# A two-block transformer kernel: the loaded tiles stand 520 bytes apart in place of 512

## What is computed

```python
def swiglu(h, w13, w2):
    gate, up = jnp.split(h @ w13, 2, axis=-1)
    return (jax.nn.silu(gate) * up) @ w2
...
    def expert_block(args):
        tok_b, e_b = args
        xb = x2[tok_b]
        return swiglu_2(xb, w1[e_b], w3[e_b], w2[e_b])
...
    y_blk = lax.map(expert_block, (buf_tok.reshape(NB, MOE_BLOCK), blk_e))
    y = y_blk.reshape(P, D) * buf_g[:, None]
    return jnp.zeros((T, D), x2.dtype).at[buf_tok].add(y)
```

## Time and profile before

| | |
|---|---|
| median of 3 runs | 3226.8 us |
| lowest, highest | 3224.2, 3227.34 us |
| the profiled execution | 3226.32 us |
| its span in the trace | 3224.4 us |
| granted TensorE clock, mean | 0.994 of full |
| PE busy | 3141.2 us, 97% of the span |
| PEld, DVE, ACT, POOL busy | 90%, 64%, 53%, 45% |

### The profile page before, as it was taken

How to read it: one execution, slowest core, us unless ns; L and a number is a source line. 1 busy time by engine, 2 the same in 40 slices (tenths; PEclk the granted TensorE clock), 3 DMA queues, 4 the chain that set the end, 5 groups by cost and what they waited for, 6 DMA issues and landing times.

```text
span 3224.4 us, 53354 instructions
## 1 busy us (share of the span) xinstructions
PE 3141.2 (97%) x20750; PEld 2887.8 (90%) x20750; DVE 2069.5 (64%) x2086; ACT 1722.8 (53%) x2031; POOL 1463.3 (45%) x587
## 2 busy tenths in 40 slices
PE   8999999999999999999999999999999999999998
PEld 8998999998789989899999998898888888888887
DVE  6644654734534376273644572657999999998997
ACT  5343444443234344644433555546777777777775
POOL 7864687882048755488888764691000000000000
PEclk9999999999999999999999999999999999999999
DMA  6443554553245443345455443356998989988985
GB/s 239 177 155 122 182 182 157 183 182 144 92 140 183 167 149 128 134 151 189 170 182 183 164 150 144 118 188 242 379 347 339 381 345 344 378 339 344 384 341 219
DMA packets 97230, 704.30 MB, mean 218 GB/s; under 512 B 10928, under 2 KB 10928, under 8 KB 11600
## 3 DMA queue, kind: packets, MB, share of 16 engines
q1 hardware_dynamic: 96768, 700.26, 58.4%
q10 hardware_dynamic: 288, 2.10, 0.2%
q0 software_dynamic: 48, 0.13, 0.0%
HBM read 701.40 MB, written 1.05 MB: 218 GB/s over the span
## 4 chain that ended last, share of the span: by engine, by line
PE 84%; DVE 7%; POOL 4%; issue 3%; ACT 2%; DVEq 0%; DMA 0%; POOLq 0%; ACTq 0%
PE bank L646 23%; PE bank L648 23%; PE bank L647 23%; POOL half_lo L608 4%; PE bank L771 3%; DVE kept L2423 2%; PE bank L1119 2%; PE bank L768 1%; PE bank L736 1%; PE bank L1261 1%; DVE expert_parts L2597 1%; PE bank L1307 1%; PE bank L889 1%; PE bank L923 1%; PE bank L785 1%
## 5 line engine op out<-in xcount | busy, mean ns | idle before, releaser
L608 POOL TENSOR_TENSOR half_lo<-ring,half_hi 128x1024 fp32r<-128x1024 f32 x582 | 1462.4, 2520 | 725.7 <-ACT half_hi L1393 721.5
L1393 ACT ACTIVATE half_hi<-ring 128x1024 fp32r<-128x1024 f32 x582 | 612.7, 1057 | 815.1 <-PE bank L648 752.1
L646 PE MATMUL bank<-h_hi,half_hi 128*128 128x256 f32 x2928 | 838.5, 286 | 10.4 <-POOL half_lo L608 10.4
L647 PE MATMUL bank<-h_lo,half_hi 128*128 128x256 f32 x2928 | 829.8, 283 | 0.0
L648 PE MATMUL bank<-h_hi,half_lo 128*128 128x256 f32 x2928 | 829.8, 283 | 0.0
L646 PEld LDWEIGHTS bank<-h_hi,half_hi 128*128 128x128 f32 x2928 | 563.3, 192 | 16.6 <-issue 8.0
L647 PEld LDWEIGHTS bank<-h_lo,half_hi 128*128 128x128 f32 x2928 | 563.3, 192 | 0.7
L648 PEld LDWEIGHTS bank<-h_hi,half_lo 128*128 128x128 f32 x2928 | 563.1, 192 | 0.0
L1846 ACT ACTIVATE expert_parts<-ring 128x1024 fp32r<-128x1024 f32 x336 | 337.3, 1055 | 109.6 <-PE bank L648 109.6
L646 PE MATMUL bank<-expert_parts,h_hi 128*128 128x512 f32 x896 | 355.1, 396 | 6.7 <-DVE expert_parts L2597 5.3
L648 PE MATMUL bank<-expert_parts,h_hi 128*128 128x512 f32 x896 | 349.9, 391 | 0.0
(11 more groups left out here) (400 smaller groups left out, 5536.7 us busy)
## 6 DMA issues: line engine op xcount, KB each, us to landing
ring<-stream SPq DMA_DIRECT2D x327, 1024.0 KB, 4.8
ring<-experts SPq DMA_DIRECT2D x168, 1024.0 KB, 6.6
kept<-experts SPq DMA_DIRECT2D x112, 1024.0 KB, 7.0
lent<-experts SPq DMA_DIRECT2D x56, 1024.0 KB, 6.8
lent<-mem ACTq DMA_DIRECT2D x2, 1024.0 KB, 6.9
con<-consts SPq DMA_DIRECT2D x1, 1505.0 KB, 12.0
kept<-x_in SPq DMA_DIRECT2D x1, 1024.0 KB, 5.0
kept<-mem SPq DMA_DIRECT2D x1, 1024.0 KB, 16.1
```

The costliest lines, as they stand in the source:

```text
L608: nc.gpsimd.tensor_tensor(half_lo[:, h % HALVES, :], ring[:, u % RING, s * HALF:(s + 1) * HALF], half_hi[:, h % HALVES, :].bitcast(F32), A ...
L646: mm(dst, w_hi, x_hi, start=start, stop=False, skip_group_check=shared)
L647: mm(dst, w_hi, x_lo, start=False, stop=False, skip_group_check=shared)
L1393: nc.scalar.activation(half_hi[:, h % HALVES, :], ring[:, u % RING, s * HALF:(s + 1) * HALF], ACT.Copy).then_inc(hi_ready, 1)
```

## The change

Three row lengths are new: `WROW` is 130 floats, `SROW` 130, and `XROW` 256, which leaves it as it was. The tiles in `half_hi` and `half_lo` stand 130 floats (520 bytes) apart in place of 128, and so do the experts' stationary tiles in `h_hi` and `h_lo`. Two floats after each tile are not used. The number of instructions, their order on each engine, their waits and their element counts stay the same. What is written to these tiles (L1393, L608, `turned`) is written in eight or four rows of 128 in place of one row of 1024 or 512; where a half moves, it moves as two rows of 128.

The tiles' starts are now spread over the multiples of 8 bytes: tile k starts 8k bytes further than before, counted from the first tile of its tensor. The tensors grow by 192 bytes each (`half_hi`, `half_lo`) and 128 bytes each (`h_hi`, `h_lo`), so what stands behind them moves too: seen modulo 512 bytes, `half_lo` starts at 192, `h_hi` at 384, `h_lo` at 0, `hid_hi`, `hid_lo`, `lent` and `expert_parts` at 128.

```diff
+WROW, XROW, SROW = PARTS + 2, TOK + 0, SLOTS + 2
...
-        half_hi = sb("half_hi", [PARTS, HALVES, HALF], F32R)
-        half_lo = sb("half_lo", [PARTS, HALVES, HALF], F32R)
-        h_hi = sb("h_hi", [PARTS, KT, TOK], F32R)
-        h_lo = sb("h_lo", [PARTS, KT, TOK], F32R)
+        half_rows = [sb(name, [PARTS, HALVES * 8 * WROW], F32R) for name in ("half_hi", "half_lo")]
+        half_hi, half_lo = (a[:, :].rearrange("p (h k c) -> p h k c", h=HALVES, k=8)[:, :, :, 0:PARTS] for a in half_rows)
+        h_rows = [sb(name, [PARTS, max(KT * XROW, 16 * SROW)], F32R) for name in ("h_hi", "h_lo")]
+        h_hi, h_lo = (a[:, 0:KT * XROW].rearrange("p (k t) -> p k t", k=KT)[:, :, 0:TOK] for a in h_rows)
...
+        slot_rows = [a[:, 0:16 * SROW].rearrange("p (k s) -> p k s", k=16)[:, :, 0:SLOTS] for a in h_rows]
+        xs_hi, xs_lo = (slot_rows[0][:, KT * i:KT * (i + 1), :] for i in range(2))
+        hT_hi, hT_lo = ([slot_rows[1][:, KT * i + 4 * j:KT * i + 4 * (j + 1), :] for j in range(2)] for i in range(2))
...
+        def by_tile(a):
+
+            return a.rearrange("p (k c) -> p k c", c=PARTS)
...
-                    nc.gpsimd.tensor_tensor(half_lo[:, h % HALVES, :], ring[:, u % RING, s * HALF:(s + 1) * HALF],
-                                            half_hi[:, h % HALVES, :].bitcast(F32), ALU.subtract).then_inc(lo_ready, 1)
+                    nc.gpsimd.tensor_tensor(half_lo[:, h % HALVES, :, :], by_tile(ring[:, u % RING, s * HALF:(s + 1) * HALF]),
+                                            half_hi[:, h % HALVES, :, :].bitcast(F32), ALU.subtract).then_inc(lo_ready, 1)
...
-                        cols = slice(k * PARTS, (k + 1) * PARTS)
-                        last = products(b[:, m * 256:m * 256 + 256], w_hi[:, cols], w_lo[:, cols], h_hi[:, k, :],
+                        last = products(b[:, m * 256:m * 256 + 256], w_hi[:, k, :], w_lo[:, k, :], h_hi[:, k, :],
                                         h_lo[:, k, :], k == 0, k == KT - 1)
...
-                            last = products(bank[5 + s][:, :], hT_hi[:, i % 2, rows_k], hT_lo[:, i % 2, rows_k],
+                            last = products(bank[5 + s][:, :], hT_hi[i % 2][:, k, :], hT_lo[i % 2][:, k, :],
                                             hi[:, cols], lo[:, cols], i == 0 and k == 0, i == NCHUNK - 1 and k == 3)
...
-                nc.scalar.activation(half_hi[:, h % HALVES, :], ring[:, u % RING, s * HALF:(s + 1) * HALF],
+                nc.scalar.activation(half_hi[:, h % HALVES, :, :], by_tile(ring[:, u % RING, s * HALF:(s + 1) * HALF]),
                                      ACT.Copy).then_inc(hi_ready, 1)
```

More of the change, by code:

```diff
@@ L515, in two_blocks @@
         onehot = page(7, 4, SLOTS)
-        scat, gate_slot = half_hi[:, 0, 0:TOK], small[:, 0:1]
+        scat, gate_slot = half_rows[0][:, 0:TOK], small[:, 0:1]
         ye_hi, ye_lo = (a[:, :, :].rearrange("p a b -> p (a b)") for a in (hid_hi, hid_lo))
         scat_bank = (2, 4, 5, 6)
[L520 to L523, removed]
+        slot_rows = [a[:, 0:16 * SROW].rearrange("p (k s) -> p k s", k=16)[:, :, 0:SLOTS] for a in h_rows]
+        xs_hi, xs_lo = (slot_rows[0][:, KT * i:KT * (i + 1), :] for i in range(2))
+        hT_hi, hT_lo = ([slot_rows[1][:, KT * i + 4 * j:KT * i + 4 * (j + 1), :] for j in range(2)] for i in range(2))
         expert_ring = [ring[:, i, :] for i in range(RING)] + [page_of[i][:, 0:UNIT] for i in (6, 9, 2)]
@@ L527, in two_blocks @@
         w_lo = [expert_parts[:, RING * UNIT:(RING + 1) * UNIT], expert_parts[:, (RING + 1) * UNIT:(RING + 2) * UNIT],
-                half_lo[:, 0:2, :].rearrange("p h c -> p (h c)")]
+                half_rows[1][:, 0:2 * HALF]]
+        def by_tile(a):
+            return a.rearrange("p (k c) -> p k c", c=PARTS)
         @block.sync
@@ L641, in half @@
                 pe.wait_ge(lo_ready, 2 * BODY * r + (h + 1))
-                return half_hi[:, h % HALVES, :], half_lo[:, h % HALVES, :]
+                return half_hi[:, h % HALVES, :, :], half_lo[:, h % HALVES, :, :]
             def products(dst, w_hi, w_lo, x_hi, x_lo, start, stop, shared=False):
@@ L674, in parted @@
                             if token_major:
-                                toks, cols = slice(m * PARTS, (m + 1) * PARTS), slice(i * 256, (i + 1) * 256)
-                                last = products(dst, x_hi[k][:, toks], x_lo[k][:, toks], w_hi[:, cols], w_lo[:, cols],
+                                toks, cols = slice(m * PARTS, (m + 1) * PARTS), slice(2 * i, 2 * i + 2)
+                                last = products(by_tile(dst), x_hi[k][:, toks], x_lo[k][:, toks], w_hi[:, cols, :], w_lo[:, cols, :],
                                                 start, stop, True)
                             else:
-                                cols = slice(i * 256 + m * PARTS, i * 256 + (m + 1) * PARTS)
-                                last = products(dst, w_hi[:, cols], w_lo[:, cols], x_hi[k], x_lo[k],
+                                last = products(dst, w_hi[:, 2 * i + m, :], w_lo[:, 2 * i + m, :], x_hi[k], x_lo[k],
                                                 start, stop, True)
@@ L703, in opening @@
                                 pe.wait_ge(xg_hi, k // 2 + 1)
-                            mm(b[:, m * 256:m * 256 + 256], half_hi[:, h % HALVES, k * PARTS:(k + 1) * PARTS], h_hi[:, k, :],
+                            mm(b[:, m * 256:m * 256 + 256], half_hi[:, h % HALVES, k, :], h_hi[:, k, :],
                                start=k == 0 and m == 0, stop=False, skip_group_check=True)
@@ L710, in opening @@
                             pe.wait_ge(xg_hi, 4 * n - 4 + k // 2 + 1)
-                        cols = slice(k * PARTS, (k + 1) * PARTS)
                         dst = b[:, m * 256:m * 256 + 256]
                         if n > 1:
-                            mm(dst, w_hi[:, cols], h_hi[:, k, :], start=k == 0 and m == 0, stop=False, skip_group_check=True)
-                        mm(dst, w_lo[:, cols], h_hi[:, k, :], start=False, stop=False, skip_group_check=True)
+                            mm(dst, w_hi[:, k, :], h_hi[:, k, :], start=k == 0 and m == 0, stop=False, skip_group_check=True)
+                        mm(dst, w_lo[:, k, :], h_hi[:, k, :], start=False, stop=False, skip_group_check=True)
                 for i, (b, u, m) in enumerate(parts):
@@ L720, in opening @@
                             pe.wait_ge(xg_lo, 4 * n - 4 + k // 2 + 1)
-                        last = mm(b[:, m * 256:m * 256 + 256], w_hi[:, k * PARTS:(k + 1) * PARTS], h_lo[:, k, :],
+                        last = mm(b[:, m * 256:m * 256 + 256], w_hi[:, k, :], h_lo[:, k, :],
                                   start=False, stop=k == KT - 1, skip_group_check=True)
@@ L823, in down @@
                         for m in range(KT):
-                            cols = slice(m * PARTS, (m + 1) * PARTS)
-                            last = products(bank[4 + m // 2][:, (m % 2) * 256:(m % 2) * 256 + 256], w_hi[:, cols], w_lo[:, cols],
+                            last = products(bank[4 + m // 2][:, (m % 2) * 256:(m % 2) * 256 + 256], w_hi[:, m, :], w_lo[:, m, :],
                                             hid_hi[:, i % 2, k * 256:(k + 1) * 256], hid_lo[:, i % 2, k * 256:(k + 1) * 256],
@@ L1889, in turned @@
                     act.wait_ge(ht_done, NCHUNK * n + 2 * c + (i + 1))
-                    nc.scalar.activation(hT_hi[:, i % 2, :], bank[4][:, :], ACT.Copy).then_inc(ht_hi_ready, 1)
+                    nc.scalar.activation(hT_hi[i % 2], by_tile(bank[4][:, :]), ACT.Copy).then_inc(ht_hi_ready, 1)
                 def chunk(i, c=0):
```

3 lines of the change are left out of this document (1 added, 2 removed).

## The result

| | before | after |
|---|---|---|
| median of 3 runs | 3226.8 us | 3203.81 us |
| lowest, highest | 3224.2, 3227.34 us | 3203.32, 3204.37 us |
| span of the profiled execution | 3224.4 us | 3201.5 us |

The ratio is 0.9931, with a 95% interval of 0.9918 to 0.9944. The kernel is 23 us faster, where 51 us were forecast. The granted clock is 0.994 in both. The time lies inside the range; it is close to the modest end of the forecast's bound (3206 us), but, as the experiments show, not for the reason that this end stood for.

A forecast was written before the change was run, and what follows sets the result against it. PE was taken as the bound, by matmul count times distance. From 3226.3 us, 51 us came off for less disturbance by loads and 0 was added for GpSimd, giving 3175 us, range 3050 to 3245 us.

The forecast's parts named there:

- the modest end of the forecast's bound: Smallest gain considered for F32R matmuls: the distance seen after a wait holds throughout, 1.7 ns less at 256 columns, 20 us.
- What bounds the kernel: PE, busy 97% of the span: matmuls times distance, with 10.8 ns extra per F32R matmul at full read rate.
- I take the last one: Main term, F32R matmuls: loads disturb streams less, 4 ns at 256 columns and 1 ns at 512, 51 us together.
- The experts, 1 ns gained a matmul: The 4032 F32R matmuls of 512 columns were each to gain 1 ns; the expert pass to shrink by 0.5 us.
- GpSimd, 0 to 5% dearer: GpSimd's subtraction L608, writing rows of 128: 2.52 to 2.65 us; 0 taken, +6 us kept for the range.
- The factor 0.87: Share of the F32R matmuls' gain that counts, 2225 of 2567 us; the rest lies beside waits for another engine.
- The sum: Whole kernel: 3226.3 us of the profiled execution, less 51, is 3175 us.
- The full gain: Rival on F32R distances: apart places remove all 10.8 ns, 167 us, so 3059 us; larger gains up to this had chance 0.22.
- Nothing: Rival on F32R distances: the 10.8 ns belong to the type at full clock, not the places; 3226 us, chance 0.17.
- The cut tiles: Rival on loads: every second tile starts 8 bytes off 16, costing 3.5 ns each; 27 us slower, 3253 us, chance 0.13.
- GpSimd as a loss: Rival: GpSimd's subtraction exceeds 2.88 us and paces every dense half; 70 us slower at 3.0 us, chance 0.04.
- The signs named ahead: Profile after: 24 L721 matmuls 2.78 us, loads 188 ns, expert pass 123.5 us, L608 and L1393 within 5%.

The follow-up runs named there:

- the series: Two kernels without the computation, rows of matmuls alone (the second with GpSimd subtractions beside them), varying starts and spacings; 256 F32R columns took 113.3 to 121.9 ns by tile start.
- the ring's 8 bytes alone: Kernel before with only `ring` starting 8 bytes on, halves unchanged modulo 256, tiles 512 bytes apart; 3213.14 us, ratio 0.9955.
- the starts alone: Changed kernel with every tensor, half and group starting as there, but tiles inside 512 bytes apart again; 3221.81 us, ratio 0.9988 against the kernel before.

## Why the prediction was off, step by step

**What bounds the kernel: right.** The time is the number of matmuls times their distance, and the change acted on that and on the engines that write the tiles. Part of the extra time at full rate does belong to the places: in the series the start of the loaded tile alone moves the distance from 113.3 to 121.9 ns, with everything else equal. That load and stream hold each other up is the simplest reading of it, not a thing that a trace shows. The Trainium skill, SBUF — State Buffer (Who interferes with whom), says that PE never waits on anyone. Whatever holds for other engines, the distance of PE's matmuls depends here on where its own two reads start.

**"I take the last one", 4 ns a matmul: the mis-sized term.** This is the step that failed first. It was put at 13,776 x 4 ns x 0.87 = 48 us and measured 13,920 x 1.82 ns = 25 us. The 4 ns came from the durations of matmuls beside which no load ran. At best that tells how much a load costs, not how much of it another start takes away. The change doesn't move the tiles to a good start; it spreads them over many, of which some give 113 and some 122 ns.

**The experts, 1 ns gained a matmul: wrong sign.** 4032 x 1 ns x 0.87 = 3.5 us of gain was forecast; measured were 4.5 ns of loss each and 13.9 us. The step took the price at 512 columns to have the same sign as at 256. The tiles already stood at a start that is best at 512 columns (0 and 256, of the nine that were run). No row of before could show that, and the range for this term should have reached as far above nothing as below.

**GpSimd, 0 to 5% dearer: wrong side.** It became 8.5% cheaper, and with it went 8.5 us of longer distances and 3.3 us in the plain forms; the ring's 8 bytes alone show that such a gain is worth about that much (12 us for 17.5%). The bound was one-sided although nothing in the trace excluded a gain. Also the cover was argued from a mean (2.52 us fits into 2.88), where 14.0 us of waits in 16 places, which a view of before shows, and 4% of the chain said that at some places it doesn't.

**The factor 0.87.** (It is 0.88 if only the matmuls of the three lines are counted.) The 25 us of undisturbed distance arrived in full, since the waits beside them shrank with the subtraction. With the subtraction unchanged they would not have: with the starts alone, 18 us of 37 came back as longer distances.

**The sum.** -25.1 - 11.8 + 13.9 = -23.0 us against the forecast's -51: half of the main term, and two terms of opposite sign that nearly cancel. That the modest end gives nearly the same total is chance.

**The rivals.** The full gain is out: no `F32R` series of 256 columns came under 113.3 ns, and all 10.8 ns gone would be 109.2. "Nothing" is out: 23 us are far beyond the noise, and the start alone moves the distance. The cut tiles are out: starts of 8, 24, 40 and 56 bytes, each off a multiple of 16, take 115.6, 121.9, 119.0 and 117.9 ns, 118.6 in the mean, and those of 0, 16, 32 and 48 bytes have the same mean. The distances after don't come in two kinds either but spread over 112 to 125 ns. GpSimd as a loss is out here, but its mechanism mattered: where the subtraction stayed at 2.52 us, part of PE's gain came back as waits.

**The signs named ahead.** Loads of 188 ns: 189. L1393 within 5%: 1061 ns. 24 matmuls in 2.78 us: 2.85. A pass of 123.5 us: 125.70. L608 within 5%: not, 2305 ns.

## What to carry to other kernels

Before choosing a layout for `F32R` matmuls, measure their distance against the starts of the loaded tile and of the moving operand, and then in the kernel itself. Here a padding that only spreads the starts gave 118.1 ns, the mean of a pattern; a gap of 64 bytes, best in the series with 113.3, gave 116.4 to 117.1 in the kernel. Try each column count by itself, since a start that saves 6.7 ns at 256 columns costs 6.0 at 512. And when PE gets faster, price the engine that feeds it both ways, cheaper and dearer: here 8 bytes between GpSimd's two inputs were worth 12 us alone and 25 us with the faster PE.

## What the runs showed of the hardware

- The distance of `F32R` matmuls with a load each depends on where the loaded tile starts. With the moving operand at a multiple of 1024 bytes and 256 columns it is 120.0 ns for a tile at 0, 113.3 at 64 and 192, 118.5 at 128, 119.8 at 256, 121.9 at 24; with 512 columns (moving operand at a multiple of 2048) 227.3 at 0, 233.3 at 64, 229.0 at 192, 226.7 at 256.
- The difference of the two starts alone doesn't set it: the moving operand 64 bytes on gives 117.8 ns where a tile 192 bytes on gives 113.3, and with the moving tiles 1032 bytes apart and the loaded ones 520 a fixed offset of 64 bytes gives 119.0.
- bf16 with 256 columns takes 109.4 ns. The Trainium skill, TensorE: Matmul & The Clock Gate (Back-to-back issue gap), gives 256 over 2.4 GHz and 2.5 ns more for an isolated matmul, 109.2 ns, and the bf16 series agrees; the best `F32R` series stays 3.9 ns above the bf16 one. What these 3.9 ns are is open.
- GpSimd's subtraction of 1024 float32 elements takes 2396 ns when both inputs start alike or 64 bytes apart, and 2002 ns when they are 8 bytes apart; the output 8 bytes on changes nothing.
- VectorE's busy time fell by 86 us in the change. Its cast into `hid_hi` went from 2369 to 1147 ns while the subtraction behind it went from 838 to 1798; their sum is 262 ns less. It goes with GpSimd's subtraction: the ring's 8 bytes alone (2075 ns) take VectorE from 2069.5 to 1881.9 us, and its L2423 (numbered as before), which reads neither `ring` nor a half, from 1610 to 1076 ns, while the experts' L2597, with GpSimd idle, keeps its 1220. How the two engines slow each other is not shown.
- Why 256 and 512 columns ask for different starts, what picks 113.3 or 117.9 ns at one offset, and what the moving operand's own start does is not settled.
